# Cache loop in groups of four value pages, with later chunk weights and six slots per state

## The reference, cut to what matters

```
h   = RMSNorm(x) @ W_in
mix = concat[ StickBreakingAttn(q,k,v) | Mamba2-SSD(z,xBC,dt) | MultiScalePool(p) ]
x   = x + mix @ W_out
x   = x + W_down( silu(causal_dwconv3(RMSNorm(x) W_gate)) * RMSNorm(x) W_up )
```

```
z = q . k * scale + head_bias
log_keep = log_sigmoid(-z), later = reversed cumsum of log_keep (without itself)
w = exp(log_sigmoid(z) + later);  o = w . v
```

## Time and profile before

| | |
|---|---|
| median of 3 runs | 3256.44 us (3252.27 to 3269.53) |
| the profiled execution, its own time | 3254.79 us |
| its span in the trace | 3253.1 us |
| mean granted clock of TensorE | 0.99 |
| PE busy | 3160.5 us (97%) |
| DVE / ACT / POOL busy | 1902.5 / 1345.9 / 427.0 us |
| chain that ended last, PE's share | 90% |
| cache loop of layer 0 | about 314 to 600 us |
| cache loop of layer 1 | about 1917 to 2208 us |

### The profile page before, as it was taken

The page is one execution under the profiler, slowest core; times in us unless marked ns, Lnnn a source line. Parts: engine busy times, 40 slices in busy tenths (PEclk is TensorE's granted clock), DMA queues, the critical chain, the costliest instruction groups (busy, mean ns, idle before and its releaser), DMA issues.

```text
span 3253.1 us, 62263 instructions
## 1 busy us (share of the span) xinstructions
PE 3160.5 (97%) x23688; PEld 3021.0 (93%) x23688; DVE 1902.5 (58%) x3325; ACT 1345.9 (41%) x1663; POOL 427.0 (13%) x541
## 2 busy tenths in 40 slices
PE   8999898999999999999999999989999999999998
PEld 7999676999999999999999986769999999999998
DVE  5574755566654665466646657555666446644664
ACT  4463666344433333233335546563443333333332
POOL 0000754210000000000300026532100000000002
PEclk9999999999999999999999999989999999999999
DMA  6443899644444444444544448986444444444443
GB/s 197 137 130 107 260 327 314 197 152 145 148 151 154 145 152 149 154 153 133 160 143 130 130 134 286 320 280 186 143 155 150 149 155 142 155 145 154 142 146 108
DMA packets 470007, 554.34 MB, mean 170 GB/s; under 512 B 21279, under 2 KB 415232, under 8 KB 469700
## 3 DMA queue, kind: packets, MB, share of 16 engines
q1 hardware_dynamic: 442339, 467.07, 45.2%
q0 software_dynamic: 27104, 84.75, 7.8%
q10 hardware_dynamic: 385, 0.14, 0.0%
HBM read 535.50 MB, written 16.38 MB: 170 GB/s over the span
## 4 chain that ended last, share of the span: by engine, by line
PE 90%; DVE 2%; DMA 2%; ACT 2%; issue 1%; POOL 1%; PEld 1%; SPq 0%; DVEq 0%; ACTq 0%; POOLq 0%; PEldq 0%
PE ps L1165 26%; PE ps L1167 26%; PE ps L1166 26%; PE ps L1409 2%; PE ps L1453 1%; PE ps L1421 1%; PE ps L1571 1%; PE ps L1561 1%; DMA kring<-in_cache_k 1%; DMA vring<-in_cache_v 1%; PE ps L1498 0%; PE ps L1435 0%; DMA raw<-in_w_out 0%; PE ps L1555 0%; ACT kT L949 0%
## 5 line engine op out<-in xcount | busy, mean ns | idle before, releaser
L1679 DVE TENSOR_TENSOR wl<-raw,wh 128x1024 fp32r<-128x1024 f32 (+1 forms) x736 | 901.8, 1235 | 985.0 <-ACT wh L782 978.4
L782 ACT ACTIVATE wh<-raw 128x1024 fp32r<-128x1024 f32 (+1 forms) x736 | 764.3, 1041 | 1585.0 <-PE ps L1167 1571.5
L1165 PE MATMUL ps<-fh,wh 128*128 128x320 f32 x2816 | 870.6, 309 | 0.0
L1166 PE MATMUL ps<-fl,wh 128*128 128x320 f32 x2816 | 870.1, 309 | 0.0
L1167 PE MATMUL ps<-fh,wl 128*128 128x320 f32 x2816 | 870.1, 309 | 0.0
L1165 PEld LDWEIGHTS ps<-fh,wh 128*128 128x128 f32 x2816 | 528.6, 188 | 0.2
L1166 PEld LDWEIGHTS ps<-fl,wh 128*128 128x128 f32 x2816 | 528.6, 188 | 0.2
L1167 PEld LDWEIGHTS ps<-fh,wl 128*128 128x128 f32 x2816 | 528.6, 188 | 0.0
L1165 PE MATMUL ps<-ah,wh 128*128 128x320 f32 x1376 | 427.0, 310 | 0.0
L1167 PE MATMUL ps<-ah,wl 128*128 128x320 f32 x1376 | 425.2, 309 | 0.0
L1166 PE MATMUL ps<-al,wh 128*128 128x320 f32 x1328 | 410.3, 309 | 0.0
(11 more groups left out here) (408 smaller groups left out, 3745.8 us busy)
## 6 DMA issues: line engine op xcount, KB each, us to landing
raw<-in_w_gate SPq DMA_DIRECT2D x88, 1024.0 KB, 5.1
raw<-in_w_up SPq DMA_DIRECT2D x88, 1024.0 KB, 5.0
raw<-in_w_in SPq DMA_DIRECT2D x72, 1024.0 KB, 5.2
kring<-in_cache_k SPq DMA_DIRECT2D x256, 256.0 KB, 4.7
vring<-in_cache_v POOLq DMA_DIRECT2D x256, 256.0 KB, 4.9
raw<-in_w_down SPq DMA_DIRECT2D x64, 1024.0 KB, 5.3
raw<-in_w_out SPq DMA_DIRECT2D x32, 1024.0 KB, 7.7
raw<-in_w_down SPq DMA_DIRECT2D x32, 768.0 KB, 4.7
```

Of the source, the lines that this page charges most:

```text
L782: act.activation(wh[:, s % 2, half, :], raw[:, s, half, :], ACT.Copy).then_inc(hi_done, 1)
L1165: pe.matmul(out, wh[:, s % 2, kk, w], hi(row), start=first, stop=False)
L1166: pe.matmul(out, wh[:, s % 2, kk, w], lo(row), start=False, stop=False)
L1679: dve.tensor_tensor(wl[:, s % 2, half, :], raw[:, s, half, :], wh[:, s % 2, half, :].bitcast(F32), ALU.subtract).then_inc(lo_done, 1)
```

## The change

On PE, a chunk time is now: two key pages and two steps, again two key pages and two steps, then four value pages, and this twice. chunk_z(qn - 1, 1) comes behind the first four value pages (slot 3), chunk_z(qn, 0) behind the second four (slot 7). weights_T(qn - 2) comes behind the second pair of key pages. On ScalarE chunk_weights(qn - 2) is at k = 1, weights_out(qn - 2) at k = 2 and chunk_logs(qn - 1) at k = 4; on VectorE relu and argument are two slots later, and the pair's mask moves from k = 7 of one chunk time to k = 1 of the next. For qn = 16 the old places are kept for the last chunk, and the weights of chunk 14 come at its start. GpSimd's value loads start four slots later. The state steps have six slots each (from slot 70), so they end at 109, and the sum is at 112. SyncE issues the loads of states 1, 2, 3 at slots 59, 63 and 67 in place of all three at 59. VectorE has one more drain.

```diff
-       57: ("T", 0, 1), 59: ("Y", 0), 60: ("N", 0, 0), 61: ("N", 0, 1), 65: ("T", 1, 0), 66: ("T", 1, 1)}
+       57: ("T", 0, 1), 59: ("Y", 0), 60: ("N", 0, 0), 61: ("N", 0, 1), 64: ("T", 1, 0), 66: ("T", 1, 1)}
 for _i in range(2, NB):
-    _s = 67 + 5 * (_i - 2)
+    _s = 70 + 6 * (_i - 2)
     MIX.update({_s: ("T", _i, 0), _s + 1: ("Y", _i - 1), _s + 2: ("T", _i, 1), _s + 3: ("N", _i - 1, 0),
                 _s + 4: ("N", _i - 1, 1)})
-MIX.update({98: ("Y", 7), 99: ("N", 7, 0), 100: ("N", 7, 1), 101: ("sum", 1)})
+MIX.update({107: ("Y", 7), 108: ("N", 7, 0), 109: ("N", 7, 1), 112: ("sum", 1)})
...
-                        if slot == SLOT["y", 2, 3] + 3:
-                            for i in range(1, 4):
+                        for i in range(1, 4):
+                            if slot == SLOT["y", 2, 3] + 4 * i - 1:
                                 state_in(i)
...
-                        if 2 <= qn <= CHUNKS:
-                            value_in(qn - 1, k)
+                        if 20 <= slot < 8 * CHUNKS + 12:
+                            value_in((slot - 12) // 8, (slot - 12) % 8)
...
+                        if qn == CHUNKS and k == 0:
+                            chunk_weights(CHUNKS - 2)
+                            weights_out(CHUNKS - 2)
...
-                        if k == 4 and qn >= 6 and qn % 4 == 2:
+                        if k == 5 and qn >= 6 and qn % 4 == 2:
                             pair_high((qn - 6) // 4)
-                        if k == 6 and 1 <= qn <= CHUNKS:
-                            chunk_weights(qn - 1)
+                        if k == 1 and 2 <= qn < CHUNKS:
+                            chunk_weights(qn - 2)
+                        if k == 2 and 2 <= qn < CHUNKS:
+                            weights_out(qn - 2)
+                        if k == 6 and qn == CHUNKS:
+                            chunk_weights(CHUNKS - 1)
...
-                        if k == 2 and 1 <= qn <= CHUNKS:
+                        if k == (2 if qn == CHUNKS else 4) and 1 <= qn <= CHUNKS:
                             chunk_logs(qn - 1)
-                    if 1 <= qn <= CHUNKS:
-                        weights_out(qn - 1)
+                    if qn == CHUNKS:
+                        weights_out(CHUNKS - 1)
...
                 for qn in range(CHUNKS + 3):
+                    if qn == CHUNKS:
+                        chunk_z(CHUNKS - 1, 1)
+                        weights_T(CHUNKS - 2)
                     for slot in range(0, 8, 2):
                         if qn < CHUNKS:
                             key_page(qn, slot)
                             key_page(qn, slot + 1)
+                        if slot == 2 and 2 <= qn < CHUNKS:
+                            weights_T(qn - 2)
+                        if slot == 4 and qn >= 6 and qn % 4 == 2:
+                            pair_fold((qn - 6) // 4)
                         step(8 * qn + slot)
-                        if 2 <= qn < CHUNKS + 2:
-                            value_page(qn - 2, slot)
-                            value_page(qn - 2, slot + 1)
-                        if slot == 0 and 1 <= qn <= CHUNKS:
-                            chunk_z(qn - 1, 1)
...
-                        if slot == 2 and qn >= 6 and qn % 4 == 2:
-                            pair_fold((qn - 6) // 4)
-                        if slot == 4 and qn < CHUNKS:
-                            chunk_z(qn, 0)
                         step(8 * qn + slot + 1)
+                        if slot % 4 == 2:
+                            if 2 <= qn < CHUNKS + 2:
+                                for page in range(slot - 2, slot + 2):
+                                    value_page(qn - 2, page)
+                            if slot == 2 and 1 <= qn < CHUNKS:
+                                chunk_z(qn - 1, 1)
+                            if slot == 6 and qn < CHUNKS:
+                                chunk_z(qn, 0)
                     if qn == CHUNKS:
                         out_step(0, 0)
-                    if 1 <= qn <= CHUNKS:
-                        weights_T(qn - 1)
+                        weights_T(CHUNKS - 1)
...
                     if s == SLOT["Y", NB - 1] + 1:
+                        dve.drain()
...
-                        if k == 3 and 1 <= qn <= CHUNKS:
+                        late = 0 if qn == CHUNKS else 2
+                        if k == 3 + late and 1 <= qn <= CHUNKS:
                             chunk_relu(qn - 1)
-                        if k == 5 and 1 <= qn <= CHUNKS:
+                        if k == 5 + late and 1 <= qn <= CHUNKS:
                             chunk_argument(qn - 1)
...
-                        if k == 7 and qn >= 5 and qn % 4 == 1:
-                            pair_mask((qn - 5) // 4)
+                        if k == 1 and qn >= 6 and qn % 4 == 2:
+                            pair_mask((qn - 6) // 4)
```

## The result

The changed kernel takes 3275.1 us in the median of 4 runs (3270.15 to 3280.51), the kernel before in the runs beside it 3256.5. The ratio is 1.0062, with a 95% interval of 1.0036 to 1.0087: slower by 0.6%, where 3232 had been forecast, in a range of 3212 to 3258. The profiled execution took 3270.15 us, its span is 3268.5.

The account below looks back on a forecast made before the run. PE's own work was taken to bound the state stretch, a late ScalarE and VectorE chain the chunks after it. Terms -9.6 - 8.2 + 4 - 9.4 - 9 + 6 + 2 = -24.2 gave 3232 us, range 3212 to 3258.

Parts of the forecast that it names:

- Value groups: PE's value pages in fours: two exits and two entries saved per chunk, 0.3 us each chunk, -9.6 us in all.
- Rival C: Value ring: pages freed in fours are loaded late, 1 us in each of 56 groups, 3288 us; chance 0.09.
- sign of being wrong: State stretch over 95 us, PE waits for value loads over 5 us a layer, or tail above 39.
- Chunk weights: Later weights: exponential waits outside the last three per layer go, -8.2 us; new waits on weight copies and banks, +4.
- State loads: SyncE's loads four slots apart: key-load waits and the clock fall behind them go, -9.4 us; shorter lead charged nothing.
- Six slots: State stretch takes one chunk more, chunks without steps fall from three to two, tail 33 us; -9 us in all.
- rival A: Chunks without steps: the chain keeps the tail, second window 38.5 us and not 33, 3243 us; chance 0.20.
- Closing part: First output products: chunk 15's weights come late as PE arrives sooner, 12 us become 15; +6 us in both layers.
- DMA, +2: State stretch: one chunk more of loads needs 359 GB/s, against 352 seen over 5 us; +2 us charged.
- rival B: State stretch: DMA becomes the bound, 94.4 us at 342 GB/s, 3239 us; chance 0.07.
- Rival D: Low clock spreads: two more falls of 8 us in each layer cost 14 us, 3246 us; chance 0.06.
- Theory G: Follow-up theory, tested by fillers in the last chunks: clock falls follow short stretches where PE idles much; 3262 to 3269 us.

Follow-up runs that it names:

- e4: The kernel before with only value pages in two groups of four and value loads four slots later; 3271.6 us, ratio 1.0045.
- e10: e7 with value pages in groups of four and value loads four slots later, chunk weights at their old places; 3257.7 us, ratio 1.0013.
- e9: The changed kernel's late weights, six slots and staggered loads, with PE's old order of pages and steps between the weights; 3261.8 us, ratio 1.0026.
- e5: The changed kernel with value pages in pairs again, behind slots 1, 3, 5 and 7; 3252.7 us, ratio 0.9988.
- e1: The kernel before with only the loads of states 1, 2, 3 staggered to slots 59, 63, 67; 3256.0 us, ratio 1.0015.
- e2: The kernel before with only six slots per state and the added drain; 3240.5 us, ratio 0.9964.
- e7: The kernel before with six slots per state, the added drain and staggered state loads; 3239.3 us, ratio 0.9959.
- e3: The changed kernel with the table of steps back at five slots per state; 3275.7 us, ratio 1.0068.
- e12: The changed kernel with unread filler transposes on PE ahead of nine waits in each layer's last three chunk times; 3268.3 us, ratio 1.0051.
- e11: The changed kernel with unread filler products on PE ahead of nine waits in each layer's last three chunk times; 3274.2 us, ratio 1.0071.

## Why the prediction was wrong, point by point

By the ratios the way from before to after is: six slots -12, stagger -2, fours +18, late weights with the order of steps that goes with them +16, together +20 us. The forecast's terms for these were -9, -9.4, -9.6 and -4.2, with +8 for the closing part and DMA. The two that came out on the other side, the value groups and the late weights, miss by 28 and 20 us. The stagger's and the late weights' figures carry some 7 and 10 us of noise.

**Value groups, -9.6: wrong, and the step that failed.** Four pages do take 0.90 us (352.90 to 353.80), as the exits and entries had it:

```profile
352.90 1.08 PE L1460 MATMUL ps<-vring,wz 128*32 128x128 f32 x32
353.80 1.04 PE L1428 MATMUL ps<-kT,qp 128*32 128x512 f32 x8
```

But the group lets four places come free at once and wants four filled at once. The term counted PE's switches and nothing for the ring, and the sum nothing for the clock; e4 and e10 measured +15 and +18 in its place. The saving itself seems to be there: PE's busy time grew by only 2.3 us (3160.5 to 3162.8) with 21 us more at the lower level, where work takes up to twice as long. That leaves an estimate of up to 8 us of switches saved.

**Rival C, the value ring late, had the mechanism, and was too dear in one way and too cheap in another.** PE waits for value loads 6.1 and 6.6 us, over the 5 a layer set as the sign of being wrong, where it waited 3.1 and 2.4 before; C had 28 a layer. What C did not price is that the waits of a group stand beside others and bring the clock down.

**Chunk weights, -8.2 and +4: wrong.** The exponential's waits fell by 2.6 and 3.4 us, not by 3.9 and 4.4: 2.6 of the 5.4 that remain in layer 0 lie in the state stretch. The new waits were sought at the copy of the weights and at the banks. They came at the key copies on VectorE, 1.0 us in layer 0 before (two waits) and 5.5 after, and at one step of the table 2.5 us (L1505 in the waits above). e9 and e5 put the whole of the late weights at +22 and +9.

**State loads, -9.4: wrong by the cover.** The key waits and the fall behind them went, but the first uses came too near in the five-slot table (e1), and the clock falls went elsewhere. "I charge nothing" for the shorter lead held with six slots alone. Measured in place of -9.4: -2 (e2 to e7), not told apart from none.

**Six slots, -9: right in size in the old order (-12), no gain seen in the new one (e3).** But the forecast had no change of the clock in this term, and 8 of the 12 us are clock loss; what brings them is not shown. The stretch was 92 us for 90. The tail was 38.8 for 33, close to rival A's 38.5 and just below the 39 of the sign of being wrong: PE waited 14.1 us in it where 10.7 were forecast, among them 2.16 and 1.73 us for key copies and 1.29 for a value load, and its first two falls cost some 2.6 (e12) where 3 us were in the sum.

**Closing part, +6: not there.** From the first output product to the value pages of chunk 15 PE took 9.1 us (581.75 to 590.83) without a wait; before it was 8.9 (573.55 to 582.45). **DMA, +2:** 346 GB/s at 1.00 busy is near rival B's 342, and 2 us is what the stretch missed by. That the DMA made these 2 us isn't shown: of the 5.8 us without PE work in the stretch, value loads have 1.1.

**Rival D had the price and not the cause.** It gave 14 us to falls of the clock; the clock loss grew by 14.0 (32.7 to 46.7). That the two agree is luck: D priced two more falls of 8 us in each layer; the profile has two more in layer 0 and three in layer 1, and most of its falls are 3.4 us long. Its cause was runs of transposes. In the changed kernel transposes ran at the lower level and the clock then rose:

```profile
328.89 1.91 PE L1416 MATMUL ps<-con,kring 128*128 128x128 f32 x8
330.60 1.88 PE L1505 MATMUL ps<-con,tk 128*128 128x128 f32 x8
332.31 0.60 PE L1406 MATMUL ps<-con,zn 128*64 128x128 f32 x4
332.75 1.06 PE L1505 MATMUL ps<-con,tk 128*128 128x128 f32 x8
```

and the filler transposes of e12 kept it up as well as products did. The Trainium skill's page "TensorE: Matmul & The Clock Gate", section "Part 4: PE-mode transpose", says that a transpose does not count as PE work for the gate in the same way; for these fp32 transposes e12 shows otherwise (.9895, against .9890 with products and .9858 without fillers), and the measurement decides.

What was missed as a whole: each wait was priced at its own length. A wait of 1.7 us that another of 1.3 follows can cost also half of the 3.4 to 6.8 us at the lower level behind them, where PE sets the pace. The forecast had this at one place, the state loads, and didn't ask it of the waits that the change makes. e11 and e12 show for the last chunk times that the falls come with such waits. That the falls ahead of them have the same cause is argued, not shown: in slots 16 to 64 the kernel before has none, the clock is 1.00,

```profile
347.00:440.00 93.00, 86.47 (x1016) 63.93 (x1015) 63.99 (x122) 64.00 (x125) 58.26 (x80) 1.00 0.88 284
```

and the changed kernel has them at 414 and 438 us, the first behind a wait of 1.12 us for a value page. The second speaks against it. PE was busy for 3.08 of the 3.4 us ahead, with 16-column products of a step Y from 435.60 on:

```profile
434.70:438.10 3.40, 3.08 (x44) 2.92 (x48) 1.13 (x3) 1.79 (x5) 3.07 (x3) 1.00 0.85 300
438.10:441.50 3.40, 3.40 (x30) 1.74 (x22) 0.00 (x0) 0.00 (x0) 1.15 (x3) 0.50 0.93 287
```

Whether the narrow products of step Y bring such falls was not tried, so part of the clock loss has an open cause.

**The sums.** 3.9 + 4.4 is 8.3 and not 8.2. The good bounds of the terms add up to -48.6 (3208 us) and not to about -42. The worse bounds add up to +23 (some 3280 us), so the terms' own bounds allowed for the measured 3275, and the stated high end of 3258 was narrower than they are.

## What to carry to other kernels

Price a wait by where it stands: in the last chunks here the granted clock fell behind short stretches with two or more waits, and work put into the waits took the falls away. Before pages of a ring are grouped for the sake of the engine that reads them, ask what it does to the ring's loads, which now come free and fall due together. When parts of a change are tried, try them alone: here one part of four was worth 12 us, and two others cost 34.

## What the runs showed that was not expected

- Filler work without a reader made a stretch shorter: 32.4 to 29.8 us with some 25% more instructions, the clock 0.84 to 1.00.
- The granted clock differs between executions of one kernel: its mean lay between .985 and .994 in 26 executions of the kernel before. Nearly the same work from 322 to 332 us ran at 0.50 in the profiled execution of the changed kernel and at 1.00 in that of the kernel before. A single profile does not give a kernel's clock loss; the table's means do.
- Six slots per state gained most of their 12 us as clock (loss 32.7 to 24.6 us).
- The clock also fell where PE had no idle time: at 514.9 and 2122.6 us of the kernel before, for 6.8 us each. Theory G leaves these out.
